# Last row block of a two-layer encoder trunk: who squares the last 256 columns, where the norm weight is multiplied in, and how the last rows are stored

## Chip, core and metric

The kernel runs on one core of one Trainium2 chip. The metric is the device time of one execution in microseconds (us), the median of several runs. A core has a matrix engine (TensorE, PE in the profile; PEld is its weight load), a vector engine (VectorE, DVE), an activation engine (ScalarE, ACT), a general engine (GpSimd, POOL) and SyncE (SP), which here only issues DMA transfers. ScalarE can issue DMA transfers too, on a queue of its own.

## What is computed

Two layers over 256 rows of 1024 columns. Each layer is a mixer (projections, two kinds of attention, an output projection), and then a gated per-layer embedding. Only the end of the second layer matters here:

```python
gate = jax.nn.sigmoid(x @ w_ple_gate[i])
e = (p[i] @ w_ple_proj[i]) * gate
x = x + _rmsnorm(e, ple_norm_g[i])       # e * rsqrt(mean(e*e) + EPS) * g
```

## The kernel before

The 256 rows are two blocks (b = 0, 1) of 128 rows, one row on each partition. A projection is computed 512 columns at a time (n = 0, 1) in a PSUM bank named `proj`; each fp32 weight is split in a high and a low part, so that a product is three matmuls (lines 1130 to 1132). All engines walk the same list of steps, `STEPS`, in its order; each executes what the step asks of it, and semaphores tie them together. Nothing is scheduled by a tool: the order on an engine is the order in the code.

The end of the list is block b = 1 of the last layer. Its columns 0 to 511 are finished by the steps `ple0` and `psq` while TensorE still computes columns 512 to 1023. Then come `last` 0, 1 and 2, for columns 512 to 1023, in two quarters of NQ = 256 columns (`tail_cols(0, ..)` and `tail_cols(1, ..)`):

- `last` 0: ScalarE takes the sigmoid of each quarter out of `proj` into `work` (line 739), VectorE multiplies it with `emb` (line 1000), which gives e. VectorE also puts the sum of squares of columns 0 to 511 plus EPS into `var[:, 1, 1]` (line 997).
- `last` 1: ScalarE squares each quarter and sums it into `tail_ssq` (line 745). VectorE multiplies quarter 0 with the norm weight `g_ple` into `e_g[1]` (a view of the buffer that the profile calls qT_a; line 1007), and then adds the three sums into `var[:, 2, 1]` (line 1011). GpSimd raises it to the power of -1/2 (`inv_sqrt`, line 519) into `rstd`.
- `last` 2: VectorE multiplies quarter 1 with `g_ple` (line 1007 again), waits for `rstd`, and computes resid = e_g * rstd + resid in two instructions of 512 columns (line 1018). SyncE waits for each of them by the semaphore `x2_done` and stores its 512 columns (line 464, 256 KB each, rows of 2 KB). Block 0 was stored in the same way some 7 us earlier.

SyncE waits for all stores by `stored`, and then all engines meet at the end of the block (line 223).

Of the kernel before, what the change touches and what calls it, by code (L numbers as in the profile page):

```python
# [22 lines left out]
P = 128  # L23
# [13 lines left out]
N = 512  # L37
# [177 lines left out]
def build(nc, x, p, pre_norm_g, w_in, w_out, post_norm_g, lambda_q1, lambda_k1, lambda_q2, lambda_k2, subln_g,  # L215
# [7 lines left out]
    with ctx:  # L223
# [203 lines left out]
        def tail_cols(q, tile):  # L427

            return tile[:, 1, N + q * NQ:N + (q + 1) * NQ]
# [4 lines left out]
        @block.sync  # L434
        def _(sp):
            def load_x(b):
                sp.dma_start(resid[:, b, :], x[0, b * P:(b + 1) * P, :]).then_inc(x_in[b], 16)

            sp.dma_start(p_raw[:, :, :], p[0, 0].rearrange("(b p) d -> p b d", p=P)).then_inc(p_in[0], 16)
            for g in range(DEPTH * U):  # L440
                L, u = divmod(g, U)
                chunk, n, k0, nk, cols = UNITS[u]
                if chunk == "PLE":
                    src = w_ple_proj[L, :, n * N:(n + 1) * N]
                elif chunk == "WO":
                    src = w_out[L, k0 * P:(k0 + nk) * P, n * N:(n + 1) * N]
                elif chunk == "WG":
                    src = w_ple_gate[L, k0 * P:(k0 + nk) * P, n * N:(n + 1) * N]
                else:
                    src = w_in[L, k0 * P:(k0 + nk) * P, COL[chunk]:COL[chunk] + cols]  # L450
                if g > LENT[-1]:
                    sp.wait_ge(lo_done, g - RAW_SLOTS + 1 if raw_turn(g)[0] > 1 else raw_turn(g)[1] + 1)
                sp.dma_start(landing(g, nk * cols).rearrange("p (k n) -> p k n", k=nk),
                             src.rearrange("(k p) n -> p k n", p=P)).then_inc(landed(g)[0], 16)

                if g == 1:
                    load_x(0)
                    load_x(1)
                elif g == 2:
                    sp.dma_start(rot_tab[:, :, :], rope.rearrange("(b p) r -> p b r", p=P)).then_inc(rope_in, 16)  # L460
            for i in range(2 * NB):
                b, n = divmod(i, 2)
                sp.wait_ge(x2_done, (DEPTH - 1) * 4 + i + 1)
                sp.dma_start(out[0, b * P:(b + 1) * P, n * N:(n + 1) * N], resid[:, b, n * N:(n + 1) * N])\
                    .then_inc(stored, 16)
            sp.wait_ge(stored, 16 * 2 * NB)


        @block.gpsimd
# [106 lines left out]
        def _(act):  # L576
# [19 lines left out]
            for pos, (L, s) in enumerate(STEPS):  # L596
# [87 lines left out]
                elif kind == "E":  # L684
                    for i in (2 * s[1], 2 * s[1] + 1):
                        g, b, maps, keys = s_task(i)
                        act.wait_ge(max_done, L * 12 + i + 1)
                        for j, m in enumerate(maps):
                            last = nc.scalar.activation(probs[:, i % 4, j * keys:(j + 1) * keys],  # L689
                                                        probs[:, i % 4, j * keys:(j + 1) * keys], ACT.Exp,  # L690
                                                        bias=neg_max[:, i % 2, j:j + 1], scale=-1.0,
                                                        accum_out=row_sum[:, g, b, m:m + 1])
                        last.then_inc(exp_done, 1)
                elif kind == "PT":
                    n = s[1]
                    act.wait_ge(tr_done, tr_index(L, s))
                    if n >= 3:
                        act.wait_ge(pv_done, L * 6 + PV_OF_PT[n - 3] + 1)
                    copy(pT[:, n % 3, :, :].rearrange("p t q -> p (t q)"), tr[:, :]).then_inc(tr_out, 1)
                elif kind == "PV":  # L700
                    for g, b, members in PV_GROUP:
                        if g == 0 and s[1] == members[-1]:
                            act.wait_ge(pv_done, L * 6 + members[-1] + 1)
                            act.wait_ge(mix_done, L * 3 + (1 if b == 0 else 3))
                            for h in range(B_HEADS):
                                last = nc.scalar.activation(y_mix[0][b][:, h, :], pv[:, h * P:(h + 1) * P],
                                                            ACT.Square, scale=row_rec[:, 0, b, 2 * h:2 * h + 1],
                                                            accum_out=ssq_h[:, b, h:h + 1])
                            last.then_inc(sqh_done, 1)
                        elif g == 1 and s[1] == members[-1]:  # L710
                            act.wait_ge(pv_done, L * 6 + members[-1] + 1)
                            copy(y_mix[1][b], pv[:, :].rearrange("p (j t) -> p j t", j=4)).then_inc(pv_out, 1)
                elif kind == "post0":
                    b, n = s[1:]
                    wait_sum(act, L, "WO", n, b)
                    if b == 1:
                        act.wait_ge(sq_done[1], L * 4 + n + 1)

                    nc.scalar.activation(gate[:, n, :], proj[bank_of("WO", n, b)][:, :], ACT.Square,
                                         scale=D_MODEL ** -0.5, accum_out=ssq[:, 1, b, n:n + 1]).then_inc(sq_done[1], 1)  # L720
                elif kind == "ple0":
                    b, n, M = s[1:]
                    wait_sum(act, M, "WG", n, b)
                    half = work[:, b, n * N:(n + 1) * N]
                    nc.scalar.activation(half, proj[bank_of("WG", n, b)][:, :], ACT.Sigmoid).then_inc(wg_sig, 1)
                elif kind == "psq":

                    b, n, M = s[1:]
                    half = work[:, b, n * N:(n + 1) * N]
                    act.wait_ge(e_done, M * 4 + 2 * b + n + 1)  # L730
                    if 2 * b + n:
                        act.wait_ge(sq_done[2], M * 4 + 2 * b + n)
                    nc.scalar.activation(gate[:, 1, :], half, ACT.Square, scale=D_MODEL ** -0.5,
                                         accum_out=ssq[:, 2, b, n:n + 1]).then_inc(sq_done[2], 1)
                elif kind == "last" and s[1] == 0:

                    wait_sum(act, L, "WG", 1, 1)
                    for q in range(2):
                        nc.scalar.activation(tail_cols(q, work), proj[bank_of("WG", 1, 1)][:, q * NQ:(q + 1) * NQ],
                                             ACT.Sigmoid).then_inc(wg_sig, 1)  # L740
                elif kind == "last" and s[1] == 1:
                    act.wait_ge(sq_done[2], L * 4 + 3)
                    for q in range(2):
                        act.wait_ge(e_done, L * 4 + 4 + q)
                        nc.scalar.activation(gate[:, 1, q * NQ:(q + 1) * NQ], tail_cols(q, work), ACT.Square,
                                             scale=D_MODEL ** -0.5, accum_out=tail_ssq[:, q:q + 1])\
                            .then_inc(sq_done[2], 1)
                elif kind == "lam":
                    act.wait_ge(lam_sum, L + 1)
                    nc.scalar.activation(lam_e[:, :], lam_s[:, :], ACT.Exp).then_inc(lam_exp, 1)  # L750
# [3 lines left out]
        def _(dve):  # L754
# [29 lines left out]
            for pos, (L, s) in enumerate(STEPS):  # L784
# [216 lines left out]
                            .then_inc(e_done, 1)  # L1001
                elif kind == "last":

                    q = s[1] - 1
                    if q == 0:
                        dve.wait_ge(e_done, L * 4 + 5)
                    nc.vector.tensor_tensor(e_g[1][:, N + q * NQ:N + (q + 1) * NQ], tail_cols(q, work),
                                            g_ple[:, N + q * NQ:N + (q + 1) * NQ], ALU.mult).then_inc(eg_done, 1)
                    if q == 0:
                        dve.wait_ge(sq_done[2], L * 4 + 5)  # L1010
                        nc.vector.tensor_scalar(var[:, 2, 1:2], tail_ssq[:, 0:1], tail_ssq[:, 1:2], var[:, 1, 1:2],
                                                ALU.add, ALU.add).then_inc(var_done[2], 1)
                        continue
                    dve.wait_ge(rstd_done[2], L * 2 + 2)
                    dve.wait_ge(eg_done, 2)
                    for n in range(2):
                        cols = slice(n * N, (n + 1) * N)
                        nc.vector.scalar_tensor_tensor(resid[:, 1, cols], e_g[1][:, cols], rstd[:, 2, 1:2],
                                                       resid[:, 1, cols], ALU.mult, ALU.add).then_inc(x2_done, 1)
                elif kind == "ple1":  # L1020
# [295 lines left out]
```

## Time and profile before

| | before |
|---|---|
| median of 3 runs | 363.35 us (363.32 to 363.58) |
| the profiled execution's own time | 363.66 us |
| its span in the trace | 361.9 us |
| PE busy | 352.1 us, 97% of the span |
| DVE, ACT, POOL busy | 265.8, 227.0, 73.3 us |
| last matmul starts | 354.61 us |
| DMA moved | 61.12 MB, of which 1.05 MB are the output |

The span runs from the first to the last instruction in the trace; the execution's own time is 1.76 us more, which lies around it. Times in the rows below are microseconds from the start of the span.

### The profile page before, as it was taken

How to read it: one execution, taken by the hardware profiler on the slowest of the kernel's cores; microseconds unless marked ns; L12 is line 12 of the kernel's file. 1: busy time of each engine (PE TensorE's matmuls, PEld its weight loads, DVE VectorE, ACT ScalarE, POOL GpSimd, SP SyncE). 2: the span in 40 equal slices, each digit the busy share in tenths (PEclk: the TensorE clock that was granted, in tenths of full speed). 3: DMA queues.
4: the chain of work that ended last, by engine and by line, in shares of the span. 5: the costliest groups of instructions: out<-in, count | busy, mean ns of one | idle time of the engine just before them, and what ended most of it. 6: DMA issues, size and time to landing. Idle time of an engine off the chain costs nothing.

```text
span 361.9 us, 5654 instructions
## 1 busy us (share of the span) xinstructions
PE 352.1 (97%) x1905; PEld 290.3 (80%) x1905; DVE 265.8 (73%) x560; ACT 227.0 (63%) x458; POOL 73.3 (20%) x121
## 2 busy tenths in 40 slices
PE   7999999999999999999999999999999999999992
PEld 6797787888888888888888878778888788888881
DVE  2886687989966676786786578878996658678543
ACT  4794566696677764664665555778577786365221
POOL 1163463061500000003015514004250000000000
PEclk9999999999999999999999999999999999999997
DMA  6994558763673455558674845447458336550011
GB/s 249 380 358 121 176 155 151 260 186 118 182 226 120 156 190 174 176 168 145 205 216 152 261 131 170 118 123 214 128 156 246 127 116 233 158 168 24 0 51 67
DMA packets 31948, 61.12 MB, mean 169 GB/s; under 512 B 2376, under 2 KB 4688, under 8 KB 31920
## 3 DMA queue, kind: packets, MB, share of 16 engines
q1 hardware_dynamic: 30784, 57.48, 50.1%
q0 software_dynamic: 1120, 3.28, 4.4%
q8 instruction: 16, 0.26, 0.3%
q14 instruction: 12, 0.10, 0.1%
q10 hardware_dynamic: 16, 0.00, 0.0%
HBM read 59.71 MB, written 1.05 MB: 168 GB/s over the span
## 4 chain that ended last, share of the span: by engine, by line
PE 92%; issue 2%; DMA 2%; ACT 1%; DVE 1%; SPq 1%; POOLq 0%; DVEq 0%; POOL 0%
PE proj L1130 26%; PE proj L1132 25%; PE proj L1131 25%; PE sc L1248 3%; PE sc L1189 3%; PE tr L1261 2%; DMA resid<-in_x_dram 2%; PE tr L1205 2%; PE pv L1282 2%; PE pv L1277 1%; PE sc L1219 1%; PE proj L1080 1%; PE proj L1089 1%; PE proj L1076 1%; PE tr L1196 0%
## 5 line engine op out<-in xcount | busy, mean ns | idle before, releaser
L1130 PE MATMUL proj<-w_hi,act_hi 128*128 128x512 f32 (+1 forms) x400 | 160.7, 402 | 0.0
L1132 PE MATMUL proj<-w_hi,act_lo 128*128 128x512 f32 (+1 forms) x400 | 155.3, 388 | 0.0
L1131 PE MATMUL proj<-w_lo,act_hi 128*128 128x512 f32 (+1 forms) x400 | 154.9, 387 | 0.0
L788 DVE TENSOR_TENSOR w_lo<-raw,w_hi 128x1024 fp32r<-128x1024 f32 (+1 forms) x102 | 122.8, 1216 | 19.1 <-ACT w_hi L578 18.1
L578 ACT ACTIVATE w_hi<-raw 128x1024 fp32r<-128x1024 f32 (+1 forms) x102 | 103.6, 1034 | 4.0 <-DMA raw<-in_w_ple_proj_dram 1.7
L1132 PEld LDWEIGHTS proj<-w_hi,act_lo 128*128 128x128 f32 x400 | 75.1, 188 | 15.8
L1130 PEld LDWEIGHTS proj<-w_hi,act_hi 128*128 128x128 f32 x400 | 75.2, 188 | 15.6 <-DVE w_lo L788 0.3
L1131 PEld LDWEIGHTS proj<-w_lo,act_hi 128*128 128x128 f32 x400 | 75.3, 188 | 13.1
L519 POOL TENSOR_TENSOR rstd<-var,minus_half 128x1 f32<-128x1 f32 x12 | 6.8, 566 | 182.1 <-DVE var L778 160.5
L689 ACT ACTIVATE probs<-probs,neg_max 128x128 f32<-128x128 f32 (+1 forms) x64 | 28.2, 446 | 1.9 <-DVE neg_max L925 1.9
L578 ACT ACTIVATE act_hi<-sc 128x512 fp32r<-128x512 f32 x20 | 11.2, 598 | 18.5 <-PE sc L1189 18.5
L578 ACT ACTIVATE pT<-tr 128x512 f32<-128x512 f32 (+1 forms) x22 | 12.7, 578 | 15.2 <-PE tr L1261 10.9
L509 POOL TENSOR_TENSOR v_all<-work,rot_tab 128x128 f32<-128x128 f32 x16 | 14.3, 896 | 33.2 <-ACT work L578 32.2
L854 DVE TENSOR_TENSOR act_lo<-sc,act_hi 128x512 fp32r<-128x512 f32 x20 | 13.2, 685 | 6.6 <-ACT act_hi L578 6.6
L541 POOL TENSOR_TENSOR rstd_h<-var_h,minus_half 128x4 f32<-128x4 f32 x4 | 6.0, 1488 | 53.3 <-DVE var_h L956 53.3
L925 DVE CUSTOM_DVE_ANT_0 probs<-sc,sel_mask 128x128 f32<-128x128 f32 (+1 forms) x32 | 9.4, 353 | 6.2 <-PE sc L1248 6.2
L578 ACT ACTIVATE work<-proj 128x512 f32<-128x512 f32 x16 | 9.6, 598 | 6.6 <-PE proj L1132 6.6
L689 ACT ACTIVATION_READ_ACCUMULATOR probs<-probs,neg_max 128x1 f32 x64 | 12.3, 192 | 0.0
L801 DVE TENSOR_TENSOR gate<-proj,gate 128x512 f32<-128x512 f32 x8 | 5.5, 690 | 8.7 <-ACT gate L632 8.7
L900 DVE MAX8 top<-score 128x8 f32<-128x128 f32 (+1 forms) x32 | 11.4, 356 | 0.5
L901 DVE MATCH_REPLACE8 score<-top,score 128x128 f32<-128x128 f32 (+1 forms) x32 | 11.0, 343 | 0.0
L1261 PE MATMUL tr<-ident,probs 128*128 128x128 f32 x72 | 10.9, 273 | 0.0
(170 smaller groups left out, 413.9 us busy)
## 6 DMA issues: line engine op xcount, KB each, us to landing
raw<-in_w_in_dram SPq DMA_DIRECT2D x59, 512.0 KB, 4.1
raw<-in_w_out_dram SPq DMA_DIRECT2D x16, 512.0 KB, 3.3
raw<-in_w_ple_gate_dram SPq DMA_DIRECT2D x16, 512.0 KB, 3.6
raw<-in_w_in_dram SPq DMA_DIRECT2D x7, 324.0 KB, 6.7
raw<-in_w_ple_proj_dram SPq DMA_DIRECT2D x4, 512.0 KB, 3.6
resid<-in_x_dram SPq DMA_DIRECT2D x2, 512.0 KB, 7.6
probs<-in_w_in_dram SPq DMA_DIRECT2D x2, 512.0 KB, 9.6
g_ple<-in_ple_norm_g_dram POOLq DMA_DIRECT2D x2, 512.0 KB, 6.8
```

Source lines behind the costliest of these rows:

```text
L509: nc.gpsimd.tensor_tensor(rot_a[:, 0:heads, :], view[:, :, 0:ROT], table(cos2, slice(0, ROT)), ALU.mult)
L578: return nc.scalar.activation(dst, src, ACT.Copy, scale=scale)
L689: last = nc.scalar.activation(probs[:, i % 4, j * keys:(j + 1) * keys], probs[:, i % 4, j * keys:(j + 1) * keys], ACT.Exp, bias=neg_max[:, ...
L788: nc.vector.tensor_tensor(w_lo[:, g % SLOTS, 0:nk * cols], landing(g, nk * cols), w_hi[:, g % SLOTS, 0:nk * cols].bitcast(fp32), ALU.subtr ...
L854: nc.vector.tensor_tensor(act_lo[:, s[2], 4 * s[3]:4 * s[3] + 4, :].rearrange("p k t -> p (k t)"), sc[i % 2][:, :], act_hi[:, s[2], 4 * s[ ...
L900: link(nc.vector.max(top8[:, :], score[b][:, :]))
L901: link(nc.vector.match_replace(score[b][:, :], top8[:, :], score[b][:, :], TAKEN))
L1130: nc.tensor.matmul(ps, src_hi[:, b, k0 + k, :], hi, start=(first_u and k == 0), stop=False)
L1131: nc.tensor.matmul(ps, src_hi[:, b, k0 + k, :], lo, start=False, stop=False)
L1132: last = nc.tensor.matmul(ps, src_lo[:, b, k0 + k, :], hi, start=False, stop=last_k)
L1189: last = nc.tensor.transpose(sc[i % 2][:, j * P:(j + 1) * P], tile, ident[:, :])
L1261: last = nc.tensor.transpose(tr[:, j * P:(j + 1) * P], probs[:, si % 4, col:col + P], ident[:, :])
```

## The change

Three things change, all in the `last` steps and in what stores their result.

1. Quarter 1 is squared and summed on VectorE, by one `tensor_tensor_reduce` whose sum starts at `var[:, 1, 1]`; ScalarE squares quarter 0 only. VectorE waits for its own instruction (`link`), and then adds two sums.
2. The product with `g_ple` is one instruction of 512 columns. It stands behind the sum in VectorE's order.
3. The last update is made in pieces of 512, 256 and 256 columns. SyncE stores the first two. ScalarE's queue stores the last 256 columns.

```diff
             for i in range(2 * NB):
                 b, n = divmod(i, 2)
                 sp.wait_ge(x2_done, (DEPTH - 1) * 4 + i + 1)
-                sp.dma_start(out[0, b * P:(b + 1) * P, n * N:(n + 1) * N], resid[:, b, n * N:(n + 1) * N])\
-                    .then_inc(stored, 16)
-            sp.wait_ge(stored, 16 * 2 * NB)
+                cols = slice(n * N, n * N + (NQ if i == 3 else N))
+                sp.dma_start(out[0, b * P:(b + 1) * P, cols], resid[:, b, cols]).then_inc(stored, 16)
+            sp.wait_ge(stored, 16 * (2 * NB + 1))
...
                 elif kind == "last" and s[1] == 1:
                     act.wait_ge(sq_done[2], L * 4 + 3)
-                    for q in range(2):
-                        act.wait_ge(e_done, L * 4 + 4 + q)
-                        nc.scalar.activation(gate[:, 1, q * NQ:(q + 1) * NQ], tail_cols(q, work), ACT.Square,
-                                             scale=D_MODEL ** -0.5, accum_out=tail_ssq[:, q:q + 1])\
-                            .then_inc(sq_done[2], 1)
+                    act.wait_ge(e_done, L * 4 + 4)
+                    nc.scalar.activation(gate[:, 1, 0:NQ], tail_cols(0, work), ACT.Square, scale=D_MODEL ** -0.5,
+                                         accum_out=tail_ssq[:, 0:1]).then_inc(sq_done[2], 1)
+                elif kind == "last" and s[1] == 2:
+                    act.wait_ge(x2_done, L * 4 + 5)
+                    act.dma_start(out[0, P:SEQ, N + NQ:D_MODEL], tail_cols(1, resid)).then_inc(stored, 16)
...
                 elif kind == "last":
 
-                    q = s[1] - 1
-                    if q == 0:
+                    if s[1] == 1:
                         dve.wait_ge(e_done, L * 4 + 5)
-                    nc.vector.tensor_tensor(e_g[1][:, N + q * NQ:N + (q + 1) * NQ], tail_cols(q, work),
-                                            g_ple[:, N + q * NQ:N + (q + 1) * NQ], ALU.mult).then_inc(eg_done, 1)
-                    if q == 0:
-                        dve.wait_ge(sq_done[2], L * 4 + 5)
-                        nc.vector.tensor_scalar(var[:, 2, 1:2], tail_ssq[:, 0:1], tail_ssq[:, 1:2], var[:, 1, 1:2],
-                                                ALU.add, ALU.add).then_inc(var_done[2], 1)
+                        link(nc.vector.tensor_tensor_reduce(out=gate[:, 1, NQ:N], in0=tail_cols(1, work),
+                                                            in1=tail_cols(1, work), scale=1.0 / D_MODEL,
+                                                            scalar=var[:, 1, 1:2], op0=ALU.mult, op1=ALU.add,
+                                                            accum_out=tail_ssq[:, 1:2]))
+                        dve.wait_ge(sq_done[2], L * 4 + 4)
+                        nc.vector.tensor_tensor(var[:, 2, 1:2], tail_ssq[:, 0:1], tail_ssq[:, 1:2], ALU.add)\
+                            .then_inc(var_done[2], 1)
                         continue
+                    nc.vector.tensor_tensor(e_g[1][:, N:D_MODEL], work[:, 1, N:D_MODEL], g_ple[:, N:D_MODEL], ALU.mult)\
+                        .then_inc(eg_done, 1)
                     dve.wait_ge(rstd_done[2], L * 2 + 2)
-                    dve.wait_ge(eg_done, 2)
-                    for n in range(2):
-                        cols = slice(n * N, (n + 1) * N)
+                    dve.wait_ge(eg_done, 1)
+                    for cols in (slice(0, N), slice(N, N + NQ), slice(N + NQ, D_MODEL)):
                         nc.vector.scalar_tensor_tensor(resid[:, 1, cols], e_g[1][:, cols], rstd[:, 2, 1:2],
                                                        resid[:, 1, cols], ALU.mult, ALU.add).then_inc(x2_done, 1)
```

VectorE's instructions at the end of the program, from the product with `emb` on; before:

```order
L1000 TENSOR_TENSOR work<-work,emb 128x256 [waits wg_sig] x2
L1007 TENSOR_TENSOR qT_a<-work,g_ple 128x256 [waits e_done]
L1011 TENSOR_SCALAR var<-ssq,var 128x1 [waits sq_done2]
L1007 TENSOR_TENSOR qT_a<-work,g_ple 128x256
L1018 SCALAR_TENSOR_TENSOR resid<-qT_a,rstd,resid 128x512 [waits eg_done,rstd_done2]
L1018 SCALAR_TENSOR_TENSOR resid<-qT_a,rstd,resid 128x512
```

The same place after the change; ISA stands for the `tensor_tensor_reduce` and the read of its sum:

```order
L1001 TENSOR_TENSOR work<-work,emb 128x256 [waits wg_sig] x2
L1007 ISA gate,ssq<-work,var 128x256 [waits e_done]
L1007 ISA ssq 128x1
L1012 TENSOR_TENSOR var<-ssq 128x1 [waits sq_done2,dve_chain]
L1015 TENSOR_TENSOR qT_a<-work,g_ple 128x512
L1020 SCALAR_TENSOR_TENSOR resid<-qT_a,rstd,resid 128x512 [waits eg_done,rstd_done2]
L1020 SCALAR_TENSOR_TENSOR resid<-qT_a,rstd,resid 128x256 x2
```

The squaring takes the place of the first product ahead of the sum, the two products have become one behind it, and the last update has a third instruction.

ScalarE's last instructions before (the sigmoids of the two quarters, then the squares):

```order
L733 ACTIVATE gate,ssq<-work 128x512 [waits sq_done2,e_done]
L739 ACTIVATE work<-proj 128x256 [waits unit_used]
L739 ACTIVATE work<-proj 128x256
L745 ACTIVATE gate,ssq<-work 128x256 [waits e_done,sq_done2]
L745 ACTIVATE gate,ssq<-work 128x256 [waits e_done]
```

And ScalarE's after the change:

```order
L733 ACTIVATE gate,ssq<-work 128x512 [waits sq_done2,e_done]
L739 ACTIVATE work<-proj 128x256 [waits unit_used]
L739 ACTIVATE work<-proj 128x256
L744 ACTIVATE gate,ssq<-work 128x256 [waits e_done,sq_done2]
L748 DMA out_dram<-resid 128x256 [waits x2_done]
```

The second square is gone, and a store that waits for VectorE's last update stands in its place.

## Rows read from the trace of the kernel before

**Rows 1.** Page, span and chain that ended last, by engine.

```profile
span 361.9 us, 5654 instructions
PE 352.1 (97%) x1905; PEld 290.3 (80%) x1905; DVE 265.8 (73%) x560; ACT 227.0 (63%) x458; POOL 73.3 (20%) x121
...
PE 92%; issue 2%; DMA 2%; ACT 1%; DVE 1%; SPq 1%; POOLq 0%; DVEq 0%; POOL 0%
```

**Rows 2.** Timeline, TensorE and ScalarE from the last matmul: start, length, instruction, idle before.

```profile
354.61 0.39 PE L1132 MATMUL proj<-w_hi,act_lo 128*128 128x512 f32 x1
355.03 0.66 ACT L739 ACTIVATE work<-proj 128x256 f32<-128x256 f32 x2 [2.25 <-PE proj L1132]
355.97 0.42 ACT L745 ACTIVATE gate<-work 128x256 f32<-128x256 f32 x1 [0.28 <-DVE work L1000]
356.29 0.19 ACT L745 ACTIVATION_READ_ACCUMULATOR gate<-work 128x1 f32 x1
356.38 0.40 ACT L745 ACTIVATE gate<-work 128x256 f32<-128x256 f32 x1
356.69 0.19 ACT L745 ACTIVATION_READ_ACCUMULATOR gate<-work 128x1 f32 x1
```

**Rows 3.** Timeline, VectorE in the same stretch.

```profile
355.79 0.42 DVE L1000 TENSOR_TENSOR work<-work,emb 128x256 f32<-128x256 f32 x1
356.24 0.42 DVE L1007 TENSOR_TENSOR qT_a<-work,g_ple 128x256 f32<-128x256 f32 x1
356.91 0.27 DVE L1011 TENSOR_SCALAR var<-ssq,var 128x1 f32<-128x1 f32 x1 [0.24 <-ACT gate L745]
357.10 0.42 DVE L1007 TENSOR_TENSOR qT_a<-work,g_ple 128x256 f32<-128x256 f32 x1
357.96 0.75 DVE L1018 SCALAR_TENSOR_TENSOR resid<-qT_a,rstd,resid 128x512 f32<-128x512 f32 x1 [0.44 <-POOL rstd L519]
358.63 0.75 DVE L1018 SCALAR_TENSOR_TENSOR resid<-qT_a,rstd,resid 128x512 f32<-128x512 f32 x1
```

**Rows 4.** Timeline, GpSimd: the power at the end, and one in block 0.

```profile
349.42 0.55 POOL L519 TENSOR_TENSOR rstd<-var,minus_half 128x1 f32<-128x1 f32 x1 [14.87 <-DVE var L778]
357.26 0.66 POOL L519 TENSOR_TENSOR rstd<-var,minus_half 128x1 f32<-128x1 f32 x1 [7.29 <-DVE var L1011]
```

**Rows 5.** Timeline, GpSimd instructions of one form twice, and VectorE's beside the slow one.

```profile
77.53 0.46 POOL L509 TENSOR_TENSOR v_all<-work,rot_tab 128x128 f32<-128x128 f32 x1
79.09 1.22 DVE L788 TENSOR_TENSOR w_lo<-raw,w_hi 128x1024 fp32r<-128x1024 f32 x1
79.25 1.39 POOL L509 TENSOR_TENSOR v_all<-work,rot_tab 128x128 f32<-128x128 f32 x1
```

**Rows 6.** Groups of VectorE by form: busy us, mean ns of one, idle before.

```profile
L925 DVE CUSTOM_DVE_ANT_0 probs<-sc,sel_mask 128x256 f32<-128x256 f32 x16 | 5.8, 421 | 6.2 <-PE sc L1248 6.2
L925 DVE DVE_READ_ACCUMULATOR2_ANT neg_max<- 128x1 f32 x64 | 5.4, 84 | 0.0
L993 DVE TENSOR_TENSOR qT_a<-work,g_ple 128x512 f32<-128x512 f32 x3 | 2.1, 692 | 0.1
L778 DVE TENSOR_SCALAR var<-ssq 128x1 f32<-128x1 f32 x7 | 1.5, 211 | 4.0 <-ACT gate L719 3.7
L781 DVE TENSOR_SCALAR var<-ssq 128x1 f32<-128x1 f32 x4 | 0.6, 151 | 1.4 <-ACT work L583 1.4
L887 DVE SCALAR_TENSOR_TENSOR score<-probs,w_idx,score 128x256 f32<-128x256 f32 x6 | 2.9, 485 | 0.2
L834 DVE SCALAR_TENSOR_TENSOR work<-resid,rstd,tr 128x512 f32<-128x512 f32 x2 | 1.5, 744 | 0.7 <-POOL rstd L519 0.7
```

**Rows 7.** Timeline and waits, SyncE: the last two stores, what its end waited for.

```profile
358.74 0.33 SPq L464 DMA_DIRECT2D out_dram<-resid  x1
359.40 0.33 SPq L464 DMA_DIRECT2D out_dram<-resid  x1
...
SPq L223 <- DMA out_dram<-resid: 1.7, 1, 1.7
```

**Rows 8.** Windows: five engines' busy us, then PEclk, DMA share, GB/s.

```profile
359.40:359.50 0.10, 0.00 (x0) 0.00 (x0) 0.00 (x0) 0.00 (x0) 0.00 (x0) 0.50 0.00 0
359.50:359.60 0.10, 0.00 (x0) 0.00 (x0) 0.00 (x0) 0.00 (x0) 0.00 (x0) 0.50 0.37 143
...
360.80:360.90 0.10, 0.00 (x0) 0.00 (x0) 0.00 (x0) 0.00 (x0) 0.00 (x0) 0.50 0.91 348
...
361.00:361.10 0.10, 0.00 (x0) 0.00 (x0) 0.00 (x0) 0.00 (x0) 0.00 (x0) 0.50 0.03 0
...
1.80:2.40 0.60, 0.37 (x1) 0.37 (x2) 0.00 (x0) 0.60 (x1) 0.14 (x1) 1.00 0.46 120
...
172.00:173.00 1.00, 1.00 (x6) 0.84 (x5) 1.00 (x3) 0.00 (x0) 0.00 (x0) 1.00 0.62 223
...
359.60:360.90 1.30, 0.00 (x0) 0.00 (x0) 0.00 (x0) 0.00 (x0) 0.00 (x0) 0.50 1.00 377
```

**Rows 9.** Timeline, the first DMA issue of ScalarE and of SyncE.

```profile
0.73 0.60 ACTq L593 DMA_DIRECT2D gate<-in_pre_norm_g_dram  x1
0.74 0.43 SPq L439 DMA_DIRECT2D p_raw<-in_p_dram  x1
```

## The prediction

> **What bounds the kernel now.** I read the page first. TensorE is busy 97% of the span and holds 92% of the chain that ended last [rows 1]; the change touches none of that. What it can move lies behind the last matmul, which starts at 354.61 and runs to 355.00 [rows 2], in a span of 361.9: 6.9 us in all. So I read the timeline of that stretch, engine by engine, and then the windows of the transfers. The reader is to see one chain, in which each step waits for the one before:
>
> - sigmoids on ScalarE from 355.03 [rows 2]; product with `emb` on VectorE, the second ending at 355.79 + 0.42 = 356.21 [rows 3];
> - the two squares on ScalarE, the second sum read at 356.69 + 0.19 = 356.88 [rows 2];
> - the sum on VectorE, 356.91 to 357.18 [rows 3];
> - the power on GpSimd, 357.26 to 357.92 [rows 4];
> - the two updates on VectorE, from 357.96; the second starts 0.67 later and ends at 359.38 [rows 3];
> - the stores, issued at 358.74 and 359.40; SyncE's end waited 1.7 us for the last, from 359.73, so it landed at about 361.43 [rows 7]. The span ends 0.47 later.
>
> I call the first update's start T; it is 357.96 now.
>
> **Part 1, the sum: where the gain seems to be.** The reduce takes the place of the first product and waits for the same thing, so it starts at 356.24 [rows 3]. The trace has the same kind of instruction at 256 columns: 421 ns, and the read of the sum 84 ns [rows 6]. The read starts some 0.08 before the main one ends, as neighbours on VectorE do (L1007 starts at 357.10, before L1011 ends at 357.18 [rows 3]). The new one takes its start value by a pointer. One pointer costs 0.06, from 151 and 211 ns of L781 and L778 [rows 6]. So the sum is there at 356.24 + 0.42 + 0.06 - 0.08 + 0.08 = 356.72, or 356.66 if the pointer is free. ScalarE's one square is there at 356.29 + 0.19 = 356.48 [rows 2], earlier. The add of two columns starts 0.03 later, as L1007 does behind L1000, at 356.75. It has no pointers; I take 0.15 of L781, with 0.21 of L778 as the other end. It ends at 356.90, against 357.18 now: 0.28 earlier.
>
> **Part 2, the product: where that gain goes.** The 512-column product takes 0.69 [rows 6]. It follows the add at 356.82 and ends at 357.51. GpSimd's power starts 0.08 behind the add, as now, at 356.98: 0.16 after the product. Now look at two things in the trace. The power took 0.55 with VectorE idle and 0.66 beside L1007 [rows 3, 4]. A GpSimd tensor_tensor took 0.46 alone, and 1.39 where a VectorE instruction with two inputs in SBUF had started 0.16 earlier; it ended at 80.64, 0.33 after that one's end at 80.31 [rows 5]. So it stood still until VectorE was through, and then needed its own time less 0.13. The last power fits: L1007 ends at 357.52, the power 0.40 later, which is 0.55 less 0.15. The order of starts is the same after the change, product first by 0.16. So the power ends 0.40 behind the product: 357.51 + 0.40 = 357.91, and T, 0.04 behind it as now, is 357.95. The product is longer by just what the add came earlier; T moves by -0.01. The bounds: a free pointer -0.06; an add of 0.21 instead of 0.15 +0.06. The product itself lies under the power, with 0.40 to spare.
>
> The Trainium skill (SBUF — State Buffer, "SBUF: two separate sides") says the same of these two engines: a VectorE instruction with two SBUF inputs and a GpSimd instruction that reads SBUF take an exclusive lock, and the later one blocks. The trace agrees (1.39 against 0.46). By that rule T stays, as in my sum; without it the power would end at 356.98 + 0.55 = 357.53 and the product would decide, which is the first rival.
>
> The sum, then, has lost ScalarE's second square (0.40 and a read), but what is late next is GpSimd, held by VectorE.
>
> **Part 3, the updates and stores.** The updates: 512 columns as now, 0.75, and then two of 256. The nearest row for 256 columns with a pointer and two inputs is L887, 485 ns [rows 6]; less the overlap of 0.08 each starts 0.40 behind the one before. The third ends at T + 0.67 + 0.40 + 0.49 = T + 1.56, against T + 1.42 now. So the last issue is 0.14 later, and carries 128 KB instead of 256.
>
> Does the smaller last transfer end earlier? The windows tell [rows 8]. The first store was issued at 358.74, its data begin to move at 359.53 or so, 0.79 later. From then to 361.0 the DMA engines hardly pause: share 1.00 and 377 GB/s over 359.60 to 360.90, and after the first tenth of a microsecond none lies under 0.91 (that at 360.80). 512 KB are 524,288 bytes; at 377 GB/s they take 1.39. The second store, issued at 359.40, could begin at 360.19, and the first is through at 359.53 + 0.70 = 360.23. So the engines are full, and the end of the data is set by the start of the first store, which the change leaves at T + 0.75, and by 512 KB, which it leaves too. After the change the third store's own path is issue at T + 1.59, data 0.79 later, 128 KB in 0.35: T + 2.73. The stream ends at 361.0 - 357.96 = T + 3.04. So the third store has 0.31 to spare, and neither its later issue nor a slower issue on ScalarE's queue (0.60 against 0.43 for SyncE at the start [rows 9]) shows. For the same reason the split gives nothing. ScalarE has nothing behind its store but the end of the block, reached some 1.3 us (T + 2.19 with an issue of 0.60, against T + 3.47) before the data have landed.
>
> What is left is the form of the pieces: the last 256 KB go in rows of 1 KB, not 2 KB. The trace shows no such store. The nearest rows are loads with rows of 1.3 KB, 223 GB/s at a share of 0.62, so 360 GB/s while busy; and the first load of the kernel, rows of 1 KB, 120 GB/s at 0.46, so 261 while busy [rows 8]. Full engines at 360 instead of 377 cost 262,144 bytes 0.03; at 261, 0.31; if the pauses stay too, 223 GB/s costs 0.48 and 120 GB/s 1.49. Below nothing I see no case, as the bytes are the same. I take 0.03, because at the end two queues feed the engines and no loads mix in, and keep the rest for the range.
>
> **Sum**, against the profiled execution: 361.9 - 0.01 + 0.03 = 361.9 of span and 363.7 of its own time. The median shown is 0.31 lower, 363.35; so I predict 363.37, rounded to 363.4. The rivals below are worked out from 363.37.
>
> **The rivals.** About 0.2% (0.73 us) is what a measurement of this kernel can tell from no change.
>
> - *GpSimd is not held* (chance 0.08). Then T is set by the product, 357.51 + 0.04 = 357.55, which is 0.40 earlier than in my sum: 362.97. Rows 4 and 5 speak against it.
> - *The last store's size counts* (0.12). If the second store now waits on something of its own rather than on full engines, the end is T + 2.73, 0.31 earlier: 363.06. For it: from issue to landing the last store takes 361.43 - 359.40 = 2.03, of which only 0.70 is its data. Against it: the windows without a pause.
> - *The reduce is slow* (0.08). The Trainium skill (Vector Engine (DVE) Microarchitecture Reference, "Points that are easy to get wrong") says that an instruction of this family halves its rate with two SBUF inputs that are not bf16. The trace does not bear it out for its neighbour: an update with both inputs in SBUF takes 0.75 [rows 3], the one with an input in PSUM 744 ns [rows 6]. As a mechanism here: 256 columns at twice the slope between 421 and 692 ns (1.06 ns a column) are 0.27 more. All behind it, product and power, is 0.27 later: 363.64.
> - *Small rows starve the stores* (0.08). This is the slower side: the last 256 KB at 120 GB/s cost 1.49 in place of my 0.03, 364.83; at 223 GB/s, 0.48, 363.82. It passes 0.73 where the rate falls under 262,144 / (0.70 + 0.73) = 183 GB/s; about half of this case.
>
> **How the numbers follow.** The sum above holds with a chance of 0.62; 0.02 is left for something outside the tail. Its own range is 363.25 to 363.75. The range over the cases reaches from the first rival, 362.97, to small rows at 223 GB/s, 363.82, and leaves out some 1 in 10. For faster by over 0.73 not even the first two rivals together suffice (0.40 + 0.31 = 0.71): 0.03. Slower by over that: half of the last rival and something for a late ScalarE queue, 0.05. Same: 0.92.
>
> **What would show it.** In the changed trace: the add starts about 0.16 earlier than L1011 did and is short; the power takes about 0.93 and ends 0.40 behind the product; the first update starts within 0.1 of 357.96; ScalarE's issue comes 1.6 behind that; the data move without a pause and end 3.0 to 3.1 behind it. A power of 0.55, or a pause in the DMA windows before the last store, would show me wrong. A reduce of 0.69 would speak for the third rival, and a share under 0.8 in the last 0.7 us of data for the fourth.

## The result, and the profile after

The changed kernel takes 364.13 us (median of 21 runs, 363.14 to 365.6), the one before 363.36 us (21 runs beside it, 362.6 to 364.09). The ratio is 1.0019, with a 95% interval of 1.0012 to 1.0026: slower by 0.77 us by the medians, by 0.69 us by the ratio. The forecast was 363.4, and the range over its cases went up to 363.82. The profiled execution is one of the quicker ones of the changed kernel: 363.61 us, with a span of 361.8.

The page's head and the last steps of the changed kernel in the timeline (start, length, instruction, idle before), the counterparts of [rows 1 to 4]:

```profile
span 361.8 us, 5656 instructions
PE 351.9 (97%) x1905; PEld 290.4 (80%) x1905; DVE 266.1 (74%) x562; ACT 226.4 (63%) x456; POOL 73.4 (20%) x121
...
354.30 0.39 PE L1134 MATMUL proj<-w_hi,act_lo 128*128 128x512 f32 x1
355.93 0.48 DVE L1007 CUSTOM_DVE_ANT_0 gate<-work,var 128x256 f32<-128x256 f32 x1
355.98 0.19 ACT L744 ACTIVATION_READ_ACCUMULATOR gate<-work 128x1 f32 x1
356.34 0.08 DVE L1007 DVE_READ_ACCUMULATOR2_ANT ssq<- 128x1 f32 x1
356.46 0.16 DVE L1012 TENSOR_TENSOR var<-ssq 128x1 f32<-128x1 f32 x1
356.54 0.69 DVE L1015 TENSOR_TENSOR qT_a<-work,g_ple 128x512 f32<-128x512 f32 x1
356.70 0.93 POOL L519 TENSOR_TENSOR rstd<-var,minus_half 128x1 f32<-128x1 f32 x1 [7.04 <-DVE var L1012]
357.67 1.54 DVE L1020 SCALAR_TENSOR_TENSOR resid<-qT_a,rstd,resid 128x512 f32<-128x512 f32 x3 [0.44 <-POOL rstd L519]
```

Count from the last matmul's start, since the stretch ahead of it differs from run to run. The sum is ready 356.62 - 354.30 = 2.32 behind it; before it was 357.18 - 354.61 = 2.57 [rows 2, 3]. So 0.25 was gained there. The power then takes 0.93 in place of 0.66, and the first update starts at 3.37, where before it was 357.96 - 354.61 = 3.35. The gain is gone before the first update.

The stores of the changed kernel, and what SyncE's end waited for (us in total, times, longest), the counterparts of [rows 7]:

```profile
358.44 0.33 SPq L465 DMA_DIRECT2D out_dram<-resid  x1
358.84 0.41 SPq L465 DMA_DIRECT2D out_dram<-resid  x1
359.24 0.38 ACTq L748 DMA_DIRECT2D out_dram<-resid  x1
...
SPq L223 <- DMA out_dram<-resid: 2.1, 1, 2.1
```

The windows of 0.60 us in which the last data move, first of the changed kernel, then of the kernel before (columns as in [rows 8]; the last two are the DMA share and GB/s):

```profile
359.97:360.57 0.60, 0.00 (x0) 0.00 (x0) 0.00 (x0) 0.00 (x0) 0.00 (x0) 0.50 1.02 335
```

```profile
360.26:360.86 0.60, 0.00 (x0) 0.00 (x0) 0.00 (x0) 0.00 (x0) 0.00 (x0) 0.50 1.05 399
```

Both are 2.30 to 2.90 behind their first update. The engines are full in both, but rows of 1 KB move at 335 GB/s here and rows of 2 KB at 399. That 399 is the best stretch of the store: over the 0.60 us from 359.60 on, where the first store's rows of 2 KB move too, it is 372.

The page rounds the span to 0.1 us. The traces hold it to the nanosecond: 361.80 changed, 361.86 before. So the tail from the last matmul's start to the end of the span is 7.50 against 7.26: 0.25 longer (the hundredths are rounded).

So one trace shows 0.25 of the 0.77. The experiments ask for both.

### The profile page after: what moved, and what is told of

Read it like the earlier page. It is cut to its first block, busy times and chain, and to the rows that moved or that the text cites. A ratio compares the mean times of both kernels' runs of the same rounds, so it can differ in the third digit from the quotient of the medians.

```text
span 361.8 us, 5656 instructions
## 1 busy us (share of the span) xinstructions
PE 351.9 (97%) x1905; PEld 290.4 (80%) x1905; DVE 266.1 (74%) x562; ACT 226.4 (63%) x456; POOL 73.4 (20%) x121
## 4 chain that ended last, share of the span: by engine, by line
PE 92%; issue 2%; DMA 2%; ACT 1%; DVE 1%; SPq 0%; POOLq 0%; POOL 0%; DVEq 0%
PE proj L1132 26%; PE proj L1134 25%; PE proj L1133 25%; PE sc L1250 3%; PE sc L1191 3%; PE tr L1263 2%; DMA resid<-in_x_dram 2%; PE tr L1207 2%; PE pv L1284 2%; PE pv L1279 1%; PE sc L1221 1%; PE proj L1082 1%; PE proj L1091 1%; PE proj L1078 1%; PE tr L1198 0%
```

## The experiments

The kernel before was run beside each group: 363.51 us (35 runs), 363.51 (35), 363.35 (35) and 363.44 (33). With 11 to 13 runs of each kernel, a comparison is good to some 0.3 to 0.4 us. The traces are sharper: the same tail came out alike within 0.02 us each time. "Tail" is always from the last matmul's start to the end of the span. The table has it for all 18 traces, in three parts, from the nanoseconds that the traces record (the last packet of the stores is the end of the data). The recorded expectations below count with the rounded 7.29 for the kernel before.

| traces | matmul to first update | first update to end of data | end of data to end of span | tail |
|---|---|---|---|---|
| before, c1, c2, c3 (three times) | 3.35 | 3.11 to 3.12 | 0.78 to 0.80 | 7.25 to 7.26 |
| changed kernel (four times) | 3.37 | 3.19 to 3.20 | 0.93 to 0.94 | 7.50 to 7.51 |
| e1 | 3.37 | 3.12 | 0.78 | 7.28 |
| e2 | 3.35 | 3.20 | 0.93 | 7.48 |
| e3 | 3.37 | 3.20 | 0.94 | 7.51 |
| e4, e7 | 3.09, 3.10 | 3.12 | 0.80, 0.79 | 7.01, 7.00 |
| e6 | 3.31 | 3.12 | 0.78 | 7.22 |
| e8 | 3.35 | 3.70 | 0.78 | 7.83 |
| e5 | 3.35 | 3.77 | 0.79 | 7.92 |

**The changed kernel again**, unedited, three more times (e0, e9, e10).

> The changed kernel once more, beside the others on one chip. Theory S (the stores cost it): slower than before by 0.5 to 1.0 us, as in the first comparison (+0.77). Theory L (the difference lies ahead of the tail, from run to run or from the place of the instructions): the difference may be anything from 0 to 0.8 us, and the tail from the last matmul on is only about 0.2 us longer in the profiled run.

> The changed kernel for the third time. The first comparison gave 0.77 us more than before, the second 0.2 to 0.35. By its tail alone 0.2. If it is 0.2 to 0.35 again, the rest of the first was chance in the first 75 us; if it is 0.5 or more, something beside the tail is slower in the changed program and is still to be found.

> The changed kernel for the fourth time, beside the three. By its tail 0.2 us slower than before; with the 0.2 to 0.3 of the earlier repeats that the tail does not explain, 0.4 to 0.5. If the idle reduce costs 0.3 and this 0.5, the two parts of the loss are found.

Measured: 363.73, 363.84 and 363.99 us, ratios 1.0007 (0.9999 to 1.0016), 1.0009 (1.0000 to 1.0019) and 1.0009 (0.9998 to 1.0019). By the medians these are 0.22, 0.49 and 0.55 us more than before, 0.42 in the mean; by the ratios 0.25, 0.33 and 0.33, 0.30 in the mean. All three tails are 0.25 longer than before. So the change comes out slower each time, by less than in the first comparison. Each interval reaches to no difference or nearly so, and by the ratios the three repeats are what the tail gives.

**Parts 1 and 2 alone** (e1), stores and update as before.

```diff
-                    for cols in (slice(0, N), slice(N, N + NQ), slice(N + NQ, D_MODEL)):
+                    for n in range(2):
+                        cols = slice(n * N, (n + 1) * N)
```

> Parts 1 and 2 only (square and sum of the last 256 columns on VectorE, one product behind the sum); update and stores as before. Theory S: the same as before within 0.15 us, with the power at 0.93 us and the first update 3.37 us behind the last matmul's start, against 3.35 before. Theory L: it carries 0.3 us or more of the difference, though its tail is as long as before.

**Part 3 alone** (e2), sum and product as before.

```diff
-                    for n in range(2):
-                        cols = slice(n * N, (n + 1) * N)
+                    for cols in (slice(0, N), slice(N, N + NQ), slice(N + NQ, D_MODEL)):
```

> Part 3 only (update in 512, 256 and 256 columns, last 256 columns stored on ScalarE's queue); sum and product as before. Theory S: slower than before by 0.5 to 1.0 us, as much as the whole change. Theory L: within 0.3 us of before, the tail longer by 0.2.

**The changed kernel with all stores on SyncE's queue** (e3).

```diff
-                    act.wait_ge(x2_done, L * 4 + 5)
-                    act.dma_start(out[0, P:SEQ, N + NQ:D_MODEL], tail_cols(1, resid)).then_inc(stored, 16)
...
+            sp.wait_ge(x2_done, (DEPTH - 1) * 4 + 5)
+            sp.dma_start(out[0, P:SEQ, N + NQ:D_MODEL], tail_cols(1, resid)).then_inc(stored, 16)
```

> The changed kernel, but SyncE issues the last 256 columns too. If the queue of ScalarE is what costs (S, queue): back to before within 0.2 us. If the rows of 1 KB cost (S, rows): slower than before by 0.5 to 1.0 us. Theory L: like the changed kernel.

Measured: e1 363.82 us (1.0005, 0.9996 to 1.0013), e2 363.91 (1.0008, 0.9999 to 1.0018), e3 364.08 (1.0017, 1.0008 to 1.0025). The tails part them better: e1 7.28, e2 7.48, e3 7.51. Parts 1 and 2 give 0.02, part 3 0.22, and it makes no difference which queue takes the last store. (That e3 comes out slower in time than the same group's run of the changed kernel, 363.73, with the same tail shows how far such a comparison scatters.) The tails are those of theory L in the expectations; a part that costs 0.5 us or more, theory S, shows in none. The window of the last data in e3 reads as in the changed kernel:

```profile
360.44:361.04 0.60, 0.00 (x0) 0.00 (x0) 0.00 (x0) 0.00 (x0) 0.00 (x0) 0.50 0.99 331
```

**Is GpSimd held by VectorE's product?** In e4 the last 512 columns of the norm weight are copied to PSUM while VectorE waits for the sigmoids; the product then has one input in SBUF. The rest is as in e1, where the power takes 0.93 like in the changed kernel. It was run twice (e4, e7). e6 does the same to the kernel before.

```diff
                     nc.vector.tensor_scalar(var[:, 1, 1:2], ssq[:, 2, 1, 0:1], EPS, None, ALU.add)
+                    link(nc.vector.tensor_copy(pv[:, :], g_ple[:, N:D_MODEL]))
...
-                    nc.vector.tensor_tensor(e_g[1][:, N:D_MODEL], work[:, 1, N:D_MODEL], g_ple[:, N:D_MODEL], ALU.mult)\
+                    nc.vector.tensor_tensor(e_g[1][:, N:D_MODEL], work[:, 1, N:D_MODEL], pv[:, :], ALU.mult)\
```

> Parts 1 and 2 with the norm weight's last 512 columns copied to PSUM while VectorE waits for the sigmoids, so that the product has one input in SBUF only; update and stores as before. If GpSimd's power is held by a VectorE instruction with two SBUF inputs: the power takes 0.55 us, not 0.93, ends 0.38 earlier, the first update starts about 3.0 us behind the last matmul's start (3.35 before), and the tail is 0.35 us shorter than before: about 6.95. If the power is slow for another reason (any VectorE work beside it): 0.93 as in the changed kernel and a tail of 7.3.

> The same kernel as e4_g_in_psum, once more, for a closer comparison with before. Its tail is 0.3 us shorter; if nothing else differs the time is 0.2 to 0.4 us less. If every edited program is late at its start by 0.2 to 0.3 us, as the comparisons so far would have it, it comes out the same as before.

> The kernel before with one thing changed: the last 512 columns of the norm weight are copied to PSUM ahead of the end, and both products read them there, so that none has two inputs in SBUF. If such an instruction holds the power: 0.55 us in place of 0.66, the tail from the last matmul's start 0.1 us shorter than 7.29, about 7.2, the time 0.1 less, which the comparison can hardly tell. Otherwise 0.66.

The timeline of e4, from the add to the first update:

```profile
354.94 0.39 PE L1133 MATMUL proj<-w_hi,act_lo 128*128 128x512 f32 x1
...
357.17 0.16 DVE L1010 TENSOR_TENSOR var<-ssq 128x1 f32<-128x1 f32 x1
357.25 0.68 DVE L1013 TENSOR_TENSOR qT_a<-work,pv 128x512 f32<-128x512 f32 x1
357.41 0.55 POOL L519 TENSOR_TENSOR rstd<-var,minus_half 128x1 f32<-128x1 f32 x1 [7.11 <-DVE var L1010]
358.03 1.41 DVE L1019 SCALAR_TENSOR_TENSOR resid<-qT_a,rstd,resid 128x512 f32<-128x512 f32 x2
```

And GpSimd's last power in e6, with VectorE's product of 256 columns beside it:

```profile
357.94 0.55 POOL L519 TENSOR_TENSOR rstd<-var,minus_half 128x1 f32<-128x1 f32 x1 [7.36 <-DVE var L1012]
```

The product starts 0.16 ahead of the power and is as long as in the changed kernel, and yet the power takes 0.55, not 0.93; in e6 0.55, not 0.66. Beside the power all that was altered is where one input lies; the copy stands ahead of it, and makes the first product with `emb` 0.07 later (0.91 behind the last matmul's start, 0.84 before). The exclusive lock that the Trainium skill describes (SBUF — State Buffer, "SBUF: two separate sides") agrees with it: a VectorE instruction with two SBUF inputs holds it against a GpSimd instruction that reads SBUF, one with a single SBUF input, outside certain fast modes, does not. The first update comes 3.09 behind the last matmul in e4 (3.35 before), and the tails are 7.01 (e4), 7.00 (e7) and 7.22 (e6) against 7.26. In the time little of it arrives: e4 363.52 us (0.9998, 0.9988 to 1.0009), e7 363.58 (1.0004, 0.9994 to 1.0014), e6 363.29 (1.0003, 0.9993 to 1.0014). A gain of 0.3 us was expected of the first two; their comparisons can't tell it from nothing, and they don't show it. No version here is shown to beat the kernel before.

**The rows or the third transfer?** e8 is the kernel before with its last store written as two pieces of 256 columns, the second first, so that it is one transfer of 256 KB with rows of 1 KB. e5 is the kernel before with its last store in two transfers of 64 rows of 2 KB each, one by SyncE and one by ScalarE at the same moment.

```diff
+                if i == 3:
+                    dst, src = (t.rearrange("p (k n) -> p k n", n=NQ)[:, ::-1, :] for t in (dst, src))
```

> The kernel before, its last 512 columns still one store by SyncE, but written as two pieces of 256 columns, the second piece first, so that its rows are of 1 KB: four stores as before, and the packets of the changed kernel. If the rows cost the 0.2 us of tail: the last 0.7 us of data at 335 GB/s in place of 390, and a tail of 7.45 to 7.5. If it is the third transfer (its own completion): full rate lost or not, a tail of 7.3 to 7.4.

```diff
+                    act.wait_ge(x2_done, L * 4 + 4)
+                    act.dma_start(out[0, P + P // 2:SEQ, N:D_MODEL], resid[P // 2:P, 1, N:D_MODEL])\
+                        .then_inc(stored, 16)
```

> The kernel before, its last 512 columns stored as two transfers of 64 rows each, one by SyncE and one by ScalarE: three stores at the end and two queues as in the changed kernel, but no rows of 1 KB. If the rows of 1 KB cost the 0.2 us of tail: data at 370 GB/s or more in each tenth of a microsecond and a tail of 7.3 us. If the third transfer or the second queue costs them: a tail of 7.45 to 7.5.

The windows of e8: the pause ahead of the last store, its data, and their end:

```profile
360.20:360.60 0.40, 0.00 (x0) 0.00 (x0) 0.00 (x0) 0.00 (x0) 0.00 (x0) 0.50 0.07 21
360.90:361.50 0.60, 0.00 (x0) 0.00 (x0) 0.00 (x0) 0.00 (x0) 0.00 (x0) 0.50 0.97 331
...
361.50:361.60 0.10, 0.00 (x0) 0.00 (x0) 0.00 (x0) 0.00 (x0) 0.00 (x0) 0.50 0.19 52
```

Its issue, in the timeline:

```profile
359.35 0.72 SPq L467 DMA_DIRECT2D out_dram<-resid  x1
```

With one transfer and one queue, rows of 1 KB again move at 331 GB/s at a share of 0.97. So the rate is the rows' doing. What it costs is best read from the packets, one for each row: those of 2 KB take 87 ns in the mean before, those of 1 KB 47 to 48 in e8 and in the traces with part 3. For 262,144 bytes each of the 16 DMA engines has 8 of the one or 16 of the other, 0.69 against 0.76 to 0.78 us. The data of the changed kernel end 0.08 later, in agreement. (The rates 399 and 335 would give 0.12, since 399 is not held over the whole store.) The tail of e8 missed its expectation of 7.3 to 7.5 (it is 7.83), since this form of transfer takes 0.72 to issue, not 0.33, and the engines pause for it. It measured 363.83 us (1.0012, 1.0003 to 1.0022).

The other 0.15 of the tail lies behind the data (last but one column of the table): 0.93 to 0.94 us in all six traces with part 3, 0.78 to 0.80 in the twelve others. Rows of 1 KB alone don't make it (e8, 0.78), and neither does a third transfer alone (e5 has one, 0.79), nor ScalarE's queue (e3, 0.94). What is left is the combination, three stores one behind the other with the last two in small rows; why it costs 0.15 is open.

e5 can't answer its question for the rate. Its windows, a pause and then the data of both transfers:

```profile
360.05:360.35 0.30, 0.00 (x0) 0.00 (x0) 0.00 (x0) 0.00 (x0) 0.00 (x0) 0.50 0.07 21
360.35:361.55 1.20, 0.00 (x0) 0.00 (x0) 0.00 (x0) 0.00 (x0) 0.00 (x0) 0.50 0.81 219
```

Two issues at the same moment took 0.55 and 0.57, where one alone takes 0.33 to 0.46, and the halves of 64 rows moved at 219 GB/s. Its tail is 7.92, and it takes 363.97 us (1.0018, 1.0005 to 1.0032).

**Is the rest in the program's start?** Compare the profiled execution of the kernel before with another of the same kernel, sent again as c1: GpSimd's first instruction on the rotary columns, the first power of the heads, and the last power. First, before:

```profile
20.63 1.46 POOL L509 TENSOR_TENSOR v_all<-v_all,rot_tab 128x96 f32<-128x96 f32 x1 [7.68 <-ACT w_idx L578]
75.61 1.95 POOL L541 TENSOR_TENSOR rstd_h<-var_h,minus_half 128x4 f32<-128x4 f32 x1 [17.73 <-DVE var_h L956]
```

And c1:

```profile
77.30 1.94 POOL L541 TENSOR_TENSOR rstd_h<-var_h,minus_half 128x4 f32<-128x4 f32 x1 [17.76 <-DVE var_h L956]
...
358.95 0.66 POOL L519 TENSOR_TENSOR rstd<-var,minus_half 128x1 f32<-128x1 f32 x1 [7.30 <-DVE var L1011]
```

The same program reached the power of the heads 1.69 us later, of which 1.60 were there at its first rotary instruction (22.23), and kept the delay to the end: from that power to the last one it is 281.65 in both (358.95 - 77.30 and 357.26 - 75.61 = 281.65). In all 18 traces the stretch from there to the last matmul is 279.0 us within 0.05. What differs from run to run is the start.

In c1 it is TensorE's clock. Two lines of the chain that ended last in c1 follow, each with two matmuls of 512 columns from the same line of the kernel, and then the windows from 8 to 9 us, before and in c1 (columns as in [rows 8]):

```profile
10.22 0.85 PE proj L1080 x2
...
13.17 0.45 PE proj L1080 x2
```

```profile
8.00:9.00 1.00, 1.00 (x7) 0.82 (x6) 0.00 (x0) 0.81 (x1) 0.00 (x0) 1.00 0.99 402
...
8.00:9.00 1.00, 1.00 (x4) 0.81 (x3) 0.88 (x2) 0.81 (x2) 0.00 (x0) 1.00 1.00 386
```

Up to 11.5 us a matmul of 512 columns starts every 0.43 us in c1, and every 0.23 from then on; before they start every 0.23 from the first ones, at 6.75, on. These are the two levels of the clock, 1.2 and 2.4 GHz. The clock column says 1.00 in both windows, but the trace's own record of the clock begins only with its rise, at 6.43 us before and at 11.53 in c1, so the column says nothing ahead of it. TensorE was busy from 2.0 us on in both but for the same pause of 0.26; why the rise came 5 us later in c1 is not shown. Eight such matmuls at 0.20 more each are 1.6 us, as much as the delay at the rotary instruction. Up to 15 us c1's chain is TensorE's work, where before it was the load of x until 10.76. In the 17 other traces the rise lies between 5.2 and 8.3 us, and the power of the heads between 75.22 and 76.21 with no such order: e0, with a rise at 7.86, reaches it at 75.37, the kernel before, with a rise at 6.43, at 75.61. So the clock explains c1, which is the slowest execution recorded of that kernel (365.36 us), and not the rest of the spread.

Controls: c2 has two more VectorE instructions behind the last update; c3 has one more `tensor_tensor_reduce` there, run three times. In them the added instructions do nothing that is asked for.

```diff
+                    nc.vector.memset(mix_c[:, 0:1], 0.0)
+                    nc.vector.memset(mix_c[:, 1:2], 0.0)
```

```diff
+                    nc.vector.tensor_tensor_reduce(out=gate[:, 1, NQ:N], in0=tail_cols(1, work),
+                                                   in1=tail_cols(1, work), scale=1.0 / D_MODEL,
+                                                   scalar=var[:, 1, 1:2], op0=ALU.mult, op1=ALU.add,
+                                                   accum_out=mix_c[:, 0:1])
```

> The kernel before, sent as if it were another, to see what the comparison makes of no change at all. Theory L (the first 75 us differ from run to run, by chance): within 0.2 us of before, up or down. If it comes out slower by 0.3 us or more, the comparison itself favours the other side.

> The kernel before, with two more VectorE instructions (memsets of one column) behind the last update, where VectorE has nothing left to do; nothing of the reference's work is changed. Theory L, by chance: within 0.2 us of before. Theory L, by the program's size or place (as in the changed kernel, which has two more VectorE instructions): slower by 0.2 to 0.5 us, all of it in the first 75 us, the tail as long as before (7.29 us from the last matmul's start).

> The kernel before, with one more tensor_tensor_reduce behind the last update, where nothing waits for it and the stores are still under way; its sum is used by nothing. Seven comparisons of programs with such an instruction in the tail came out 0.13 to 0.59 us slower than their tails explain, six without it -0.12 to 0.19. If the presence of this instruction in the program makes the first 75 us later: slower than before by 0.3 us, in this and its two repeats. If that pattern was chance: within 0.15 us of before in their mean.

> The same kernel again, with the same expectations; the three together tell 0.3 us from nothing.

> The same kernel again, with the same expectations; the three together tell 0.3 us from nothing.

Measured: c1 363.41 us (1.0000, 0.9990 to 1.0009), c2 363.47 (0.9997, 0.9987 to 1.0007); c3 363.56, 363.29 and 363.88 (1.0004, 0.9989 and 1.0001), in the mean of the ratios 0.9998. Within what such a comparison can tell, it favours no side, more instructions alone cost nothing, and the presence of the reduce does not either. The pattern that led to c3 was chance, or has another cause.

## Why the prediction was wrong

**Part 1** was right: the reduce took 0.48 (0.42 + 0.06 for the pointer), the add 0.16. The sum was forecast 0.28 earlier and came 0.25 earlier.

**Part 2** was right, and e4, e7 and e6 show its mechanism by taking the held input away. The power was forecast at 0.93 and took 0.93; the first update moved by 0.02, forecast -0.01. The first and the third rival fell. The forecast was off by 0.03 in both parts, within what its rows allow.

**Part 3** had the mechanism right: the data are one stream without a pause, ScalarE's queue doesn't show (e3), and the smaller last store ends nothing earlier, so that the second rival fell. The size was wrong, and this is the step that failed. "Full engines at 360 instead of 377 cost 262,144 bytes 0.03" took for rows of 1 KB a rate of loads with rows of 1.3 KB in mid-kernel; the rows of 1 KB cost 0.08 (e8, and the end of the data). And the sum had no term for what follows the data: it took the time from their end to the end of the span as fixed, and that grew by 0.15 with part 3 (e2, e3), for a reason that stays open. The fourth rival names small rows, which is right for the 0.08, but its mechanism, pauses between them, isn't there: the engines are full at 1.02. The tail grew by 0.25 in place of 0.02.

**The sum** missed a term ahead of the tail. With 0.25 the kernel would be at 363.61, inside the range. It was 0.77 slower in the first comparison (0.69 by the ratio, with an interval from 0.44 to 0.94) and in three repeats 0.42 in the mean by the medians, 0.30 by the ratios. The forecast took the stretch ahead of the last matmul as fixed, from three runs within 0.26 us; 156 further runs of the same kernel lie between 362.6 and 364.5, the 13 of c1 go up to 365.36, and the start varies by up to 1.7 us between traces of it. So the larger part of the first 0.77 has no place in the tail, and the repeats don't bear it out; chance in the start is the likely cause, but no trace of the slow runs of that comparison was taken, and it isn't shown. The number of instructions (c2) and the reduce (c3) showed no cost as causes; nothing in a trace of the changed kernel shows one, as its four profiled executions are at the power of the heads at 75.30, 75.37, 75.57 and 75.74, and the one before at 75.61.

## What to carry to other kernels

When a step ahead of GpSimd is made faster, look at what VectorE does while GpSimd works: an instruction with two SBUF inputs that starts first decides when GpSimd ends, and one input in PSUM frees it. At the end of a kernel, where transfers already follow each other without a pause, a smaller last store with shorter rows only added time here. And before a forecast of a tenth of a microsecond is compared with a median, look at how much the start of the same program varies, and read TensorE's clock there from the distance of its matmuls.

## What the runs showed of the hardware that was not expected

Stores to memory in rows of 1 KB moved at 331 to 338 GB/s with all DMA engines busy, rows of 2 KB at 355 to 375 in the first store and at 393 to 406 in the best 0.6 us of the second; a packet of 1 KB took 47 to 48 ns in the mean, one of 2 KB 87. Two stores of 64 rows issued at once by SyncE and ScalarE took 0.55 and 0.57 us to issue, against 0.33 for one of 128 rows, and moved at 219 GB/s. A store whose two pieces run backwards took 0.72 us to issue. The stretch of 279 us between the first head power and the last matmul repeats within 0.05 us, while the first 21 us of the same program differed by 1.6 between two traces. TensorE's clock rose at 5.2 to 8.3 us in 17 traces and at 11.5 in one, with the same work behind it, and the clock column of the windows shows neither.
